# Expert feed-forward of a hybrid decoder layer: the down bias is added before the weight splits at a tile's end, and the first down weights are split after the first chunk's clipping

## What is computed

```
logits = (t @ w_router + b_router);  top_v, top_i = lax.top_k(logits, 4);  gates = softmax(top_v)
gu    = lax.ragged_dot(xs, w_gu, sizes) + b_gu[e_sorted]
x_glu = jnp.minimum(gu[:, :D_FF], 7.0)
x_lin = jnp.clip(gu[:, D_FF:], -7.0, 7.0)
act   = x_glu * jax.nn.sigmoid(1.702 * x_glu) * (x_lin + 1.0)
out   = lax.ragged_dot(act, w_down, sizes) + b_down[e_sorted]
out   = out * gates.reshape(-1)[order][:, None]
y     = jnp.zeros_like(t).at[tok].add(out)
```

## Time and profile before

| | |
|---|---|
| median of 3 runs | 5674.24 us (5672.62 to 5676.24) |
| profiled execution, its own time | 5676.82 us |
| its span in the trace | 5675.2 us |
| PE busy | 5272.8 us, 93% of the span |
| PEld busy | 4680.6 us, 82% |
| DVE busy | 3105.4 us, 55% |
| ACT busy | 1728.8 us, 30% |
| POOL busy | 987.1 us, 17% |

### The profile page before, as it was taken

The page is one execution under the profiler, slowest core; times in us unless marked ns, Lnnn a source line. Parts: engine busy times, 40 slices in busy tenths (PEclk is TensorE's granted clock), DMA queues, the critical chain, the costliest instruction groups (busy, mean ns, idle before and its releaser), DMA issues.

```text
span 5675.2 us, 81720 instructions
## 1 busy us (share of the span) xinstructions
PE 5272.8 (93%) x30128; PEld 4680.6 (82%) x30128; DVE 3105.4 (55%) x5828; ACT 1728.8 (30%) x2756; POOL 987.1 (17%) x829
## 2 busy tenths in 40 slices
PE   8999999986996997869699999999999999999997
PEld 7888888876884886758599899899989999999997
DVE  4313130006664666625455666666677777777776
ACT  4112111110102664113232333333333344444343
POOL 0000000003310200212312231313132222222221
PEclk9999999995557998989799999999999999999999
DMA  3122221210003434434345454545456666666665
GB/s 138 67 76 72 72 76 67 78 72 5 0 0 119 142 125 146 157 137 135 115 171 170 149 185 151 191 149 190 154 191 221 212 218 220 221 219 218 219 219 186
DMA packets 237535, 802.38 MB, mean 141 GB/s; under 512 B 32503, under 2 KB 52623, under 8 KB 201521
## 3 DMA queue, kind: packets, MB, share of 16 engines
q1 hardware_dynamic: 198960, 673.21, 32.1%
q0 software_dynamic: 32656, 106.62, 7.9%
q10 hardware_dynamic: 5760, 20.45, 1.1%
HBM read 652.88 MB, written 147.89 MB: 141 GB/s over the span
## 4 chain that ended last, share of the span: by engine, by line
PE 44%; DVE 4%; ACT 1%; issue 1%; DMA 0%; POOL 0%; DVEq 0%; ACTq 0%; POOLq 0%
PE ex_g L1892 27%; PE ex_d L1906 15%; DVE ex_y L2041 2%; PE ex_g L1878 1%; ACT ex_wgh L1945 1%; DVE ex_wdl L1999 1%; DVE ex_wgl L1993 1%; DVE ex_t L2020 0%; DVE ex_bgu L2014 0%; DMA ex_xg<-h_d,ex_nxt 0%; POOL ex_y L1848 0%; DMA ex_nxt<-slots_d 0%; ACT ex_xh L1958 0%; POOL out L1851 0%; DVEq L2052 0%
## 5 line engine op out<-in xcount | busy, mean ns | idle before, releaser
L1892 PE MATMUL ex_g<-ex_xh,ex_wgh 128*128 128x256 f32 (+2 forms) x4352 | 1292.3, 297 | 71.9 <-DVE ex_t L2020 64.5
L1892 PE MATMUL ex_g<-ex_xh,ex_wgl 128*128 128x256 f32 (+2 forms) x4352 | 1284.3, 295 | 0.0
L1892 PE MATMUL ex_g<-ex_xl,ex_wgh 128*128 128x256 f32 (+2 forms) x4352 | 1284.2, 295 | 0.0
L1892 PEld LDWEIGHTS ex_g<-ex_xh,ex_wgh 128*128 128x128 f32 x4352 | 823.4, 189 | 101.6 <-issue 71.1
L1892 PEld LDWEIGHTS ex_g<-ex_xl,ex_wgh 128*128 128x128 f32 x4352 | 823.8, 189 | 8.5
L1892 PEld LDWEIGHTS ex_g<-ex_xh,ex_wgl 128*128 128x128 f32 x4352 | 824.6, 189 | 0.0
L1993 DVE TENSOR_TENSOR ex_wgl<-ex_wg,ex_wgh 128x2048 fp32r<-128x2048 f32 x274 | 626.6, 2287 | 54.8 <-ACT ex_wgh L1945 52.2
L1945 ACT ACTIVATE ex_wgh<-ex_wg 128x2048 fp32r<-128x2048 f32 x274 | 524.4, 1914 | 394.2 <-PE ex_g L1892 366.8
L1848 POOL TENSOR_SCALAR ex_y<-ex_y,ex_cur 128x1024 f32<-128x1024 f32 x82 | 294.9, 3597 | 1601.2 <-DVE ex_y L2041 1601.2
L1906 PE MATMUL ex_d<-ex_wdh,ex_ath 128*128 128x512 f32 x1312 | 523.4, 399 | 0.0
L1906 PE MATMUL ex_d<-ex_wdl,ex_ath 128*128 128x512 f32 x1312 | 515.7, 393 | 0.0
(11 more groups left out here) (354 smaller groups left out, 8656.8 us busy)
## 6 DMA issues: line engine op xcount, KB each, us to landing
ex_wg<-in_w_gu SPq DMA_DIRECT2D x276, 1024.0 KB, 5.6
ex_wd<-in_w_down SPq DMA_DIRECT2D x276, 512.0 KB, 6.3
qkv_d<-prj_o SPq DMA_DIRECT2D x144, 256.0 KB
att_blk<-qkv_d SPq DMA_DIRECT2D x48, 768.0 KB, 4.2
prj_raw<-in_w_in SPq DMA_DIRECT2D x112, 256.0 KB, 3.6
ex_bd<-in_b_down SPq DMA_DIRECT2D x34, 512.0 KB
gate_d<-prj_o SPq DMA_DIRECT2D x64, 256.0 KB
mix_ring<-gate_d SPq DMA_DIRECT2D x32, 512.0 KB, 3.8
```

What stands on the lines that cost most here:

```text
L1892: last = pe.matmul(gu[j][:, 0:size], w[:, k, j, :], x[:, k, 0:size], start=(k == 0 and x is xh and w is h), stop=(k == KD - 1 and w is l))
```

## The change

Two pieces of VectorE's program move. The additions of the down bias become a function `add_bias`, called in the last chunk right after `save_x`, ahead of the two splits. And `split_down` for chunk 0 of a tile is no longer issued at the end of the tile before (nor ahead of the first loop), but within chunk 0, behind its two clippings. No instruction is added or removed, except one wait that gets a slot of its own in place of another.

```diff
                         tsc(t2[z][:, w], gu[1][:, w], bgu[:, NF + f:NF + f + 1], LIMIT + 1.0, ALU.add,
                             ALU.min).then_inc(gu_read, 1)
+                        if f == 0:
+                            split_down(NF * i, 0, 0)
                         dve.wait_ge(sig, NF * i + f + 1)
...
                         if f == NF - 1:
                             save_x(i + 1, nb)
+                            add_bias(i, nb)
                         split_gate_up(NF * i + f + 2, z, (f + 2) % RAW)
-                        split_down(NF * i + f + 1, 1 - z, (f + 1) % RAW)
+                        if f < NF - 1:
+                            split_down(NF * i + f + 1, 1 - z, (f + 1) % RAW)
+
+                def add_bias(i, nb):
                     dve.wait_ge(bd_in, 16 * i + 16)
                     dve.wait_ge(y_free, i + 1)
                     dve.wait_ge(down_mm, NF * i + NF + 1)
...
                 split_gate_up(0, 0, 0)
                 save_x(0, B6)
-                split_down(0, 0, 0)
                 split_gate_up(1, 1, 1)
```

## The result

The changed kernel takes 5594.89 us (median of 4 runs, 5593.82 to 5600.25), the kernel before 5675.24 us in the runs beside it. The ratio is 0.9861, with a 95% interval of 0.9843 to 0.9878: 80 us or 1.4% faster. The forecast was 5592. The profiled execution took 5593.82 us, 83.0 less than the 5676.82 of the profiled one before, where the sum had 82.6; its span is 5592.1 us.

A forecast was written before the change was run, and what follows sets the result against it. PE was taken to stall at 33 tile borders on VectorE's late clipping. Savings 2.3 + 25.9 + 2.7 + 32.3 + 4.4 + 15 = 82.6 us from 5676.8, less 2.6, gave 5592 us; range 5583 to 5618 at 0.85.

The forecast's parts named there:

- T: The end of VectorE's last xl operation at a tile border, from which the prediction counts its times in us.
- MIDDLE borders: Eleven borders ahead of MIDDLE tiles: the whole stall of PE, 2.35 us each, goes; 25.9 us saved.
- MIDDLE to SMALL: The one border between these tile sizes: 1.0 of 3.7 us of stall stays, 2.7 us saved.
- SMALL borders: 19 borders between SMALL tiles: 2.0 us of stall each, 0.3 returns ahead of gate_up 2, 32.3 us saved.
- tail: Last tile's additions, scalings and scatters on GpSimd start 4.4 us earlier, saving 4.4 us.
- The stall is VectorE's lateness: At 33 tile borders PE waits ahead of gate_up 1 for VectorE's clipping of chunk 0, 69.7 us.
- Hindrance one: At SMALL borders GpSimd's first scaling now lies under VectorE's large split, which loses 0.1 us, within 0.18 to spare.
- Hindrance two: At SMALL borders GpSimd's second scaling delays chunk 0's small split; 0.3 us of stall returns ahead of gate_up 2.
- The clock: Half-speed PE clock stretches after nine stalls, ten units of 3.4 us at 1.5 us each, vanish: 15 us saved.
- Rival one: GpSimd's second scatter holds chunk 2's large split up to 1.2 us ahead of gate_up 2: 5615 us, chance 0.18.
- Rival two: GpSimd's scaling blocks VectorE's two-input splits for its whole length; SMALL borders save nothing: 5638 us, chance 0.10.
- Rival three: Chunk 4's later refill on SyncE delays following weight loads; slower, 5694 us if landing takes 21 us, chance 0.02.

## Why the prediction was right

By stages, from one border's T to another's in the two profiled executions:

| stretch | forecast saving | measured |
|---|---|---|
| LARGE borders (2) | 2.3 | 2.5 |
| MIDDLE borders (11), with 5 clock stretches at 1.5 | 25.9 + 7.5 = 33.4 | 34.2 |
| MIDDLE to SMALL, with the double stretch | 2.7 + 3.0 = 5.7 | 5.4 |
| SMALL borders (18), with 2 clock stretches | 30.6 + 3.0 = 33.6 | 31.2 |
| last tile and tail, with 1 clock stretch | 1.7 + 1.5 + 4.4 = 7.6 | 7.5 |
| all ahead of the first border | 0 | 2.2 |
| sum | 82.6 | 83.0 |

**The stall is VectorE's lateness, and both parts shorten it.** Right: the waits fell as written, and no MIDDLE or LARGE stall is left. At the MIDDLE to SMALL border 1.0 was forecast to stay; by start times 1.2 - 0.12 = 1.1 stayed.

**Hindrance one, the large split under the first scaling.** Right in size (0.1 forecast, 0.08 measured) and in kind: the experiment with the split inside the scaling gave the moment of release again, 1.9 us before the end of the scaling's row.

**Hindrance two, the small split under the second scaling.** Right: "about 2.6 us" was 2.73, clipping 1 at T + 14.05 against T + 14.2. Mis-sized is what returns as stall, 0.3 forecast and 0.44 measured, 2.7 us in 19 borders. The clipping let PE go at T + 14.66 instead of T + 14.8, but PE arrived sooner still, at T + 14.22 instead of T + 14.5. Most of that is a misreading of the earlier trace rows: its 5.89 us run to the modelled end of the last matmul, while the next one already starts 5.73 us after the first, as PE's timeline of the kernel before shows. The prediction made this correction for the stalls, but not here.

```profile
4442.58 0.39 PE L1906 MATMUL ex_d<-ex_wdh,ex_ath 128*128 128x512 f32 x1
```

**The clock.** Right: all nine stretches went, one of them of double length, at 1.5 us for each 3.4, the price that the MIDDLE tiles of the kernel with the additions alone show by themselves.

**Rival one** did not happen: the large split of chunk 2 started 0.02 us ahead of the second scatter (4390.37 and 4390.39) and took 2.35. **Rival two** is refuted for the large split by the experiment with the split inside the scaling, and for the small one by its 2.73 us in the changed kernel. The Trainium skill's rule, page "SBUF — State Buffer", section "Who interferes with whom", that whoever issues first has the shared ports for the whole instruction and the other waits, agrees with the lengths of most copies (4.22 and 3.34 us, to the scaling's end) and not with the splits. **Rival three**: the refill is issued later as forecast, and PE has no wait for it.

**What the prediction did not see** is how near the change lies to losing its gain. The sum treats the bias operations as 0.44 us and the high-part copy as 0.3; they are that only because both fall outside GpSimd's scalings. The runs with one part alone show that the same reasoning gave 58 and 55 us for them where 30 and 6 were measured: the step that failed there is that I took the copies' lengths as fixed and applied the scaling's hindrance to two-input operations alone. The trace of before had the warning, beside the very rows that the prediction read. The first line is the high-part copy of chunk 1 at the SMALL border, the second the bias copy at the MIDDLE one:

```profile
4444.22 0.99 DVE L2030 CAST ex_ath<-ex_at 128x256 fp32r<-128x256 f32 x1
4025.11 0.79 DVE L2014 COPY ex_bgu<-ex_bin 128x8 f32<-128x8 f32 x1
```

The first ended 0.15 us behind the scaling's end at 4445.06 and took 0.99 us instead of 0.29. In that trace 44 of the 272 such copies took longer than 0.5 us, and all 44 ended 0.1 to 0.2 us behind a scaling's end. That the whole change came out right owes something to where its copies happened to fall.

**The 2.2 us ahead of the first border** are not the change's. The first LARGE tile took 106.0 us before and 103.2 after. The granted clock at its start is the difference, in the kernel before (first line) and in the changed one:

```profile
2842.20:2848.20 6.00, 6.00 (x19) 0.50 1.00 410
```

```profile
2842.80:2848.80 6.00, 6.00 (x35) 1.00 1.02 415
```

PE's clock was at half for most of the 55 us ahead of the experts, where PE had little to do (in the changed kernel it was busy for 5.6 of 41 us there). In the profiled execution of before a half-clock stretch reached 6.2 us into the first tile, in that of the changed kernel the last one had ended ahead of it. The other kernels follow the same line: no half clock in the first tile, 103.2 us (five of them); 3.1 to 4.4 us of it, 104.6 to 105.2 us (three, the one with ScalarE among them). Their orders of VectorE's work do not sort them so. So 2.8 us of the 83.0 are luck of the two executions, less the 0.6 us by which the changed kernel came later to the experts, and the sum's 82.6 stands against 80.8 from the first border on and 80.3 between the medians. The SMALL borders lack 2.4 us of their forecast, the MIDDLE ones gave 0.8 more.

## What to carry to other kernels

When an engine's queue is reordered, ask of each operation not only how long it takes but what it will now lie beside: here 8-element operations at the MIDDLE borders decided some 25 us in one kernel and most of 79 us in another. A part of a change tested alone can look worthless (6 us) and still be needed for the whole (80 us), if the other part moves it out of a collision. And where GpSimd's work holds up a critical VectorE queue, look for an engine that is idle at that moment: here the multiplication on ScalarE gave 10 us.

## What the runs showed of the hardware

GpSimd's scaling of 128 x 1024 floats (2.85 us alone) held VectorE's operations with two inputs in memory, where it held them, only until 1.7 to 1.9 us before the end of its row: 34 large splits took 2.96 us instead of 2.28, 31 small splits of the changed kernel up to 2.76 instead of 1.22. A copy or cast from memory to memory, even of 8 elements for each partition, was mostly held until the row's end: 3.34 and 4.22 us instead of 0.16 and 0.29. This is no rule without exceptions. The 8-element copy at 4435.78 in the earlier trace rows began 0.89 us into a scaling and took 0.24, and in the kernels with the small split alone and with the split inside the scaling 24 casts that stood right behind a held two-input operation took their normal 0.29 to 0.33 us, although they began 1.4 us before the scaling's end. The 8-element operation of 1.59 us was released when the two-input ones are, 1.87 us before the end.

What decides which operation is held is open as well. A two-input operation that began 0.02 us ahead of a scatter, or 0.18 and 0.38 us after it, was not held; but the product in the earlier trace rows, which also began 0.38 us after its scatter (4026.75), was. In the kernels with the small split alone and with the split inside the scaling 24 products that began 0.1 to 0.3 us into a scaling were not held either, and the large split that began 0.3 us into one was. All moments of release are counted from the ends of GpSimd's rows; what the engine does inside one no run here shows.
